# The opening of an encoder kernel: cross-attention key weights loaded as quarters of the inputs instead of one head at a time

## The chip, the cores and the metric

The kernel runs on one core of a Trainium2 chip. The metric is the time of one execution on the device, in microseconds (us). A core has a matrix engine (TensorE, PE in the profile), a vector engine (DVE), a scalar engine (ACT), a sync engine (SP) that here issues nearly all DMA transfers, and 16 DMA engines. Each engine runs its own list of instructions in order. The engines meet only through semaphores.

## The reference, cut to what matters

The program is one layer of a hybrid encoder on 256 tokens of 2048 features. Only its opening is touched by the change. The opening computes, from a second input `mem` (256 tokens of 2048 features), the keys and values of a cross-attention that is used much later:

```python
m = rmsnorm(mem, norm_mem)
kv = (m @ cross_wkv).reshape(1, 256, 2, 4, 128)   # cross_wkv: 2048 x 1024
k, v = kv[:, :, 0], kv[:, :, 1]                   # 4 heads of 128 features each
```

Columns 0 to 511 of `cross_wkv` give the keys, one head per 128 columns, and columns 512 to 1023 give the values. After that the main input `x` is normalised in the same way and multiplied by `w_in`, and the mixers, the output projection, the cross-attention and the feed-forward part follow. All of it is in float32 at full accuracy.

## The kernel before, in words

**Split products.** The kernel multiplies in the format fp32r and keeps the accuracy of float32 by splitting each operand into a high part (a rounding copy) and a low part (operand minus high part), and a product takes three matmuls: high x high, high x low and low x high (`three`, lines 1252 to 1260). A weight chunk is 128 partitions x 2048 floats, 1 MB. For each chunk SP loads it into one of three slots of `raw`, ACT writes the high part `hi` (`split` in the scalar block, line 375), DVE writes the low part `lo` (`split` in the vector block, line 746), and PE multiplies. PE asks for a chunk with `ready(n)`, which waits for the semaphore `lo_ready` that DVE raises. SP may reload a slot when DVE is done with it (`raw_free`), and ACT and DVE may overwrite `hi` and `lo` when PE has finished the chunk three places back (`products_done`).

**The activations.** `mem` is split in the same way, but has to be transposed first, since features must lie on partitions. Features are taken in eight groups of 256 (two 128-blocks k each). `turn_group` (line 1306) has PE transpose a group into a PSUM bank, `token_hi` (line 405) has ACT write the high part times the norm's gain into `uh`, and `token_lo` (line 782) has DVE write the low part into `ul`. The factor 1/rms of each token is applied after the products: DVE computes it (`tile_squares` line 767, `token_rsqrt` line 760 and the lines of `newton`), PE spreads it over the partitions (`spread_scale`, line 1332), and DVE multiplies each head's key block by it when it takes the block out of PSUM (`take_key`, line 864).

**The order of the opening before.** Chunks 0 to 3 are one head each: all 2048 input features x 128 key columns. A DMA of such a chunk reads pieces of 512 bytes. SP issues the four quarters of `mem` with the two halves of chunk 0 between them, waits until all of `mem` has landed, and then issues chunks 1, 2 and 3, the tables and vectors, `x`, and the value chunks 4 to 7. PE turns all eight groups first, each into a bank of its own, and then computes one head after the other, each over all 16 blocks k, into its own bank. The six small transposes of gain and bias vectors (line 1426) follow head 2, and the spreading of 1/rms stands in the middle of it. ACT and DVE split the activations of all groups around the two halves of chunk 0, then chunks 1, 2 and 3 as whole chunks. DVE computes the squares and 1/rms of `mem` between chunks 1 and 3, and those of `x` after chunk 3, with the four `take_key` between the other steps.

**The value part, and what follows.** Chunks 4 to 7 hold quarters of the input features x 512 value columns (pieces of 2048 bytes). `row_product` (lines 1255 to 1257) multiplies each into banks 4 and 5. After each of them PE turns two groups of `x` (`turn_scaled`, line 1325) into the banks that `X_BANKS` names; ACT and DVE split these. In DVE's list, a chain of 18 small operations for the rotary angles (lines 879 to 898) stands between the split of chunk 5 and the split of chunk 6. From chunk 8 on the projection by `w_in` runs one 128-column tile after the other.

The order of all work is written out by hand in one list per engine. No planner decides it.

Of the kernel before, what the change touches and what calls it, by code (L numbers as in the profile page):

```python
# [16 lines left out]
F32, F32R, I32 = mybir.dt.float32, mybir.dt.float32r, mybir.dt.int32  # L17
ALU, ACT, AX = mybir.AluOpType, mybir.ActivationFunctionType, mybir.AxisListType

P = 128  # L20
T = 256
# [70 lines left out]
def products(n):  # L92

    extra = {N_U: 3, N_U + 1: 3, N_U + 2: 6, N_U + 3: 1}
    return n + 1 + sum(v for m, v in extra.items() if m <= n)
# [25 lines left out]
def encoder(nc, x, mem, positions, norm_mix, w_in, mla_q_norm, mla_w_uq, mla_kv_norm, mla_w_ukv, mla_out_norm,  # L121
# [4 lines left out]
    with ctx:  # L126
# [5 lines left out]
        def S(name):  # L132

            if name not in signals:
                signals[name] = Signal(ctx.enter_context(nc.semaphore(name)))
            return signals[name]
# [95 lines left out]
        def _(sp):  # L232
            def raw_free(n):

                sp.wait_ge(S("lo_ready").sem, n - RING + 1)

            def load(n, src, shape, slot=None, off=0):
                slot = n % RING if slot is None else slot
                size = int(np.prod(shape))
                dst = raw[:, slot, off:off + size]  # L240
                if len(shape) == 2:
                    dst = dst.rearrange("p (a b) -> p a b", b=shape[1])
                    sp.dma_start(dst, src).then_inc(S(f"raw_landed{slot}").sem, 16)
                else:
                    dst = dst.rearrange("p (a b c) -> p a b c", b=shape[1], c=shape[2])
                    sp.dma_start(dst, src).then_inc(S(f"raw_landed{slot}").sem, 16)

            def rows(w):
                return w[0].rearrange("(k p) c -> p k c", p=P)

            for q in range(4):
                sp.dma_start(mems[:, :, q * 512:(q + 1) * 512],
                             mem[0].rearrange("(t p) d -> p t d", p=P)[:, :, q * 512:(q + 1) * 512]).then_inc(S(f"mem_landed{q}").sem, 16)
                if q % 2:
                    half = q // 2
                    sp.dma_start(raw[:, 0, half * CH // 2:(half + 1) * CH // 2].rearrange("p (a b) -> p a b", b=P),
                                 rows(cross_wkv)[:, half * KD // 2:(half + 1) * KD // 2, 0:P]).then_inc(
                                     S("raw_landed0" if half else "first_landed").sem, 16)
            for q in range(4):
                sp.wait_ge(S(f"mem_landed{q}").sem, 16)  # L260
            load(1, rows(cross_wkv)[:, :, P:2 * P], (KD, P))
            load(2, rows(cross_wkv)[:, :, 2 * P:3 * P], (KD, P))
            raw_free(3)
            load(3, rows(cross_wkv)[:, :, 3 * P:4 * P], (KD, P))
# [3 lines left out]
            for v, n in ((norm_mix, 16), (norm_cross, 16), (norm_ffn, 16), (mla_q_norm, 4),  # L268
                         (mla_kv_norm, 2), (mla_out_norm, 6), (ssm_norm, 6), (swa_out_norm, 4), (ssm_conv_b, 10)):
                sp.dma_start(vrows[at_row:at_row + n, 0, :], v.rearrange("l (r c) -> (l r) c", c=P)).then_inc(vectors, 16)  # L270
                at_row += n
            sp.dma_start(vrows[0:40, 1, :], ssm_conv_w[0].rearrange("k (r c) -> (k r) c", c=P)).then_inc(vectors, 16)
# [3 lines left out]
            for t in range(TT):  # L276
                sp.dma_start(xs[:, t, :], x[0, t * P:(t + 1) * P, :]).then_inc(S("x_landed").sem, 16)
            sp.dma_start(posi.bitcast(I32), positions[0].partition_broadcast(P)).then_inc(S("pos_landed").sem, 16)
            sp.dma_start(small[:, s_dall:s_dall + SSM_H], ssm_d[0].partition_broadcast(P)).then_inc(S("params_landed").sem, 16)
            sp.dma_start(small[:, s_sink:s_sink + SWA_H], swa_sinks[0].partition_broadcast(P)).then_inc(S("params_landed").sem, 16)  # L280
            sp.dma_start(row12[:, 0:1], ssm_dt_bias.rearrange("l h -> h l")).then_inc(S("params_landed").sem, 16)
            sp.dma_start(row12[:, 1:2], ssm_a_log.rearrange("l h -> h l")).then_inc(S("params_landed").sem, 16)

            for g in range(4):
                raw_free(N_XV + g)
                load(N_XV + g, rows(cross_wkv)[:, 4 * g:4 * g + 4, 512:1024], (4, 512))
# [79 lines left out]
        def _(act):  # L366
# [34 lines left out]
            def token_hi(name, g, g_col, b):  # L401

                act.wait_ge(S(f"{name}_turned").sem, g + 1)
                for k in (2 * g, 2 * g + 1):
                    a.mark(act.activation(uh[:, k, :], bank[b][:, (k % 2) * T:(k % 2 + 1) * T], ACT.Copy,
                                          scale=vecs[:, g_col + k:g_col + k + 1]), S(f"{name}_hi"))
# [62 lines left out]
            for g in range(4):  # L469
                token_hi("mem", g, V_MEM, g)  # L470
            act.wait_ge(S("first_landed").sem, 16)
            a.mark(act.copy(hi[:, 0, 0:CH // 2], raw[:, 0, 0:CH // 2]), S("first_hi"))
            for g in (4, 5):
                token_hi("mem", g, V_MEM, g)
            act.wait_ge(S("raw_landed0").sem, 16)
            a.mark(act.copy(hi[:, 0, CH // 2:], raw[:, 0, CH // 2:]), S("hi_ready"))
            for g in (6, 7):
                token_hi("mem", g, V_MEM, g)

            split(1)  # L480
            a.mark(act.activation(junk, mems[:, 0, :], ACT.Square, accum_out=small[:, s_ss:s_ss + 1]), S("mem_ss"))
            split(2)
            token_root("mem")
            split(3)
            act.wait_ge(S("vecs_turned").sem, 2)
            a.mark(act.copy(vecs[:, 0:V_MEM], bank[3][:, 0:V_MEM]), S("vecs_ready"))
            a.settle()
            act.wait_ge(S("x_landed").sem, 32)
            a.mark(act.activation(junk, xs[:, 0, :], ACT.Square, accum_out=small[:, s_ss:s_ss + 1]), S("x_ss"))
            token_root("x")  # L490
            split(4)
# [239 lines left out]
        def _(dve):  # L731
# [3 lines left out]
            def go(ins, signal=None):  # L735
                d.mark(ins, signal or step)
                d.settle()
# [101 lines left out]
            for g in range(4):  # L839
                token_lo("mem", g, V_MEM, g)  # L840
# [3 lines left out]
            for g in (4, 5):  # L844
                token_lo("mem", g, V_MEM, g)
# [3 lines left out]
            for g in (6, 7):  # L849
                token_lo("mem", g, V_MEM, g)  # L850
            split(1)
            tile_squares("mem", mems)
            split(2)
# [3 lines left out]
            split(3)  # L857
            dve.wait_ge(S("mem_spread").sem, 1)
            go(dve.tensor_copy(mem_scale, bank[4][:, 0:T]))

            def take_key(n):

                dve.wait_ge(S("products_done").sem, products(n))
                d.mark(dve.tensor_tensor(kxT[:, n, :], bank[KEY_BANKS[n]][:, 0:T], mem_scale, ALU.mult), S("key_taken"))

            dve.wait_ge(S("x_landed").sem, 32)
            take_key(0)
# [3 lines left out]
            take_key(1)  # L871
            split(4)
            take_key(2)
            split(5)
            take_key(3)
# [369 lines left out]
        def _(pe):  # L1245
# [162 lines left out]
            for g in range(8):  # L1408
                pe.wait_ge(S(f"mem_landed{g // 2}").sem, 16)
                if g == 7:  # L1410
                    pe.wait_ge(S("vecs_ready").sem, 1)
                turn_group("mem", mems, g, g)
            for n in range(N_XK, N_XK + 4):
                if n == 0:
                    pe.wait_ge(S("first_lo").sem, 1)
                    tile_product(n, n, lo_signal="mem_lo", ks=(0, KD // 2))
                    ready(n)
                    tile_product(n, n, lo_signal="mem_lo", ks=(KD // 2, KD))
                else:
                    ready(n)  # L1420

                    tile_product(n, KEY_BANKS[n], mid=(lambda: spread_scale("mem", mem_diag, 4)) if n == 2 else None)
                if n == 2:
                    pe.wait_ge(S("vectors_landed").sem, N_VECTORS)
                    for k, (r, col) in enumerate(((V_ROWS_A, 0), (40, V_CW), (88, V_FW), (88, V_FW + 88), (88, V_FW + 176), (88, V_FB))):
                        last = pe.transpose(bank[3][:, col:col + r], vrows[0:r, k, :], tab[0:r, C_ID:C_ID + r])
                    last.then_inc(S("vecs_turned").sem, 1)
            for n in range(N_XV, N_XV + 4):
                ready(n)
                g = n - N_XV  # L1430
                row_product(n, uh, ul, 4 * g, 4, g == 0, g == 3)
                if g == 0:
                    pe.wait_ge(S("key_taken").sem, 2)
                    pe.wait_ge(S("vecs_ready").sem, 2)
                if g == 1:
                    pe.wait_ge(S("key_taken").sem, 4)
                if g == 2:
                    pe.wait_ge(S("x_lo").sem, 2)
                if g == 3:
                    pe.wait_ge(S("x_lo").sem, 6)  # L1440
                for gg in (2 * g, 2 * g + 1):
                    turn_scaled("x", xs, x_diag, gg, X_BANKS[gg])
# [285 lines left out]
KEY_BANKS = (0, 1, 2, 7)  # L1728
X_BANKS = (1, 3, 6, 7, 0, 1, 3, 6)
# [11 lines left out]
def z_bank(n):  # L1741
    return n % 3 if n < N_U else (n - N_ZB + 1) % 3

# [52 lines left out]
```

## Time and profile before

| | us |
|---|---|
| median of 3 runs | 1234.81 (1234.19 to 1234.86) |
| the profiled execution | 1234.29 |
| its span in the trace | 1232.5 |
| PE busy | 1200.0 (97% of the span) |
| DVE busy | 884.7 (72%) |
| ACT busy | 655.8 (53%) |
| mean granted clock of TensorE | 0.991 of full speed |

The span is the time from the first to the last recorded instruction; the execution's own time is 1.8 us longer. "Busy" counts the time in which an engine executes something. Start times in all views count from the span's start. The value chunks' matmuls begin at 44.88 us, so the change touches about the first 4% of the span directly.

### The profile page before, as it was taken

How to read it: one execution, taken by the hardware profiler on the slowest of the kernel's cores; microseconds unless marked ns; L12 is line 12 of the kernel's file. 1: busy time of each engine (PE TensorE's matmuls, PEld its weight loads, DVE VectorE, ACT ScalarE, POOL GpSimd, SP SyncE). 2: the span in 40 equal slices, each digit the busy share in tenths (PEclk: the TensorE clock that was granted, in tenths of full speed). 3: DMA queues.
4: the chain of work that ended last, by engine and by line, in shares of the span. 5: the costliest groups of instructions: out<-in, count | busy, mean ns of one | idle time of the engine just before them, and what ended most of it. 6: DMA issues, size and time to landing. Idle time of an engine off the chain costs nothing.

```text
span 1232.5 us, 18921 instructions
## 1 busy us (share of the span) xinstructions
PE 1200.0 (97%) x7020; PEld 1049.7 (85%) x7020; DVE 884.7 (72%) x1243; ACT 655.8 (53%) x866; POOL 0.2 (0%) x4
## 2 busy tenths in 40 slices
PE   7899999999999999999999999999999999999995
PEld 6799999988887888888888888888888888888884
DVE  6763888777476557877767767777777777777775
ACT  6444764475534557646454545555454545454444
POOL 0000000000000000000000000000000000000000
PEclk9999999999899999999999999999999999999998
DMA  8776756442555545766665758575757566575842
GB/s 254 238 180 171 182 155 178 118 114 70 205 171 171 171 137 141 224 185 174 200 192 165 200 168 224 174 204 170 204 172 202 170 191 188 169 202 168 222 152 69
DMA packets 309932, 217.07 MB, mean 176 GB/s; under 512 B 11414, under 2 KB 272254, under 8 KB 309246
## 3 DMA queue, kind: packets, MB, share of 16 engines
q1 hardware_dynamic: 309710, 216.31, 60.7%
q8 instruction: 30, 0.49, 0.2%
q10 hardware_dynamic: 176, 0.14, 0.1%
q14 instruction: 16, 0.13, 0.0%
HBM read 214.33 MB, written 2.10 MB: 176 GB/s over the span
## 4 chain that ended last, share of the span: by engine, by line
PE 92%; DVE 3%; ACT 2%; DMA 2%; issue 1%; SPq 0%; ACTq 0%; DVEq 0%
PE bank L1282 25%; PE bank L1283 12%; PE bank L1255 10%; PE bank L1256 10%; PE bank L1257 10%; PE bank L1258 6%; PE bank L1259 6%; PE bank L1260 6%; PE bank L1286 2%; DVE lo L746 1%; PE bank L1367 1%; DMA raw<-in_cross_wkv_dram 1%; ACT hi L375 1%; PE bank L1398 1%; PE bank L1285 1%; DMA arena<-in_mem_dram 1%
## 5 line engine op out<-in xcount | busy, mean ns | idle before, releaser
L746 DVE TENSOR_TENSOR lo<-raw,hi 128x2048 fp32r<-128x2048 f32 x196 | 448.8, 2290 | 151.1 <-ACT hi L375 143.3
L1282 PE MATMUL bank<-ux,hi 128*128 128x512 f32 x1320 | 470.1, 399 | 0.9 <-DVE arena L1202 0.9
L375 ACT CAST hi<-raw 128x2048 fp32r<-128x2048 f32 x196 | 373.5, 1911 | 111.1 <-PE bank L1257 100.8
L1283 PE MATMUL bank<-ux,lo 128*128 128x256 f32 x1320 | 370.7, 281 | 0.0
L1282 PEld LDWEIGHTS bank<-ux,hi 128*128 128x128 f32 x1320 | 248.0, 188 | 58.7 <-issue 1.2
L1283 PEld LDWEIGHTS bank<-ux,lo 128*128 128x128 f32 x1320 | 249.2, 189 | 4.0
L1255 PE MATMUL bank<-hi,ch 128*128 128x512 f32 x472 | 186.2, 395 | 1.7 <-DVE cl L1142 1.4
L1256 PE MATMUL bank<-lo,ch 128*128 128x512 f32 x472 | 184.7, 391 | 0.0
L1257 PE MATMUL bank<-hi,cl 128*128 128x512 f32 x472 | 184.6, 391 | 0.0
L1258 PE MATMUL bank<-ux,hi 128*128 128x256 f32 (+1 forms) x592 | 170.7, 288 | 1.7 <-DVE lo L746 1.7
L1259 PE MATMUL bank<-ux,hi 128*128 128x256 f32 (+1 forms) x592 | 167.5, 283 | 0.0
L1260 PE MATMUL bank<-ux,lo 128*128 128x256 f32 (+1 forms) x592 | 167.4, 283 | 0.0
L705 ACT COPY arena<-bank 128x256 f32<-128x256 f32 x88 | 32.8, 373 | 208.6 <-PE bank L1286 208.6
L1258 PEld LDWEIGHTS bank<-ux,hi 128*128 128x128 f32 (+1 forms) x592 | 112.9, 191 | 5.2 <-issue 2.4
L1259 PEld LDWEIGHTS bank<-ux,hi 128*128 128x128 f32 (+1 forms) x592 | 112.9, 191 | 0.1
L1260 PEld LDWEIGHTS bank<-ux,lo 128*128 128x128 f32 (+1 forms) x592 | 112.8, 191 | 0.0
L1255 PEld LDWEIGHTS bank<-hi,ch 128*128 128x128 f32 x472 | 89.5, 190 | 20.2 <-DVE cl L1142 1.8
L1257 PEld LDWEIGHTS bank<-hi,cl 128*128 128x128 f32 x472 | 89.6, 190 | 18.9
L1256 PEld LDWEIGHTS bank<-lo,ch 128*128 128x128 f32 x472 | 89.7, 190 | 18.4
L1183 DVE SCALAR_TENSOR_TENSOR arena<-arena,vecs 128x255 f32<-128x255 f32 (+1 forms) x176 | 85.1, 484 | 25.9 <-DVE arena L1202 4.4
L1201 DVE TENSOR_TENSOR arena<-bank,arena 128x256 f32<-128x256 f32 x88 | 37.1, 422 | 62.5 <-ACT arena L705 62.1
L1119 DVE TENSOR_TENSOR arena<-arena,bank 128x512 f32<-128x512 f32 x96 | 60.7, 680 | 0.9 <-PE bank L1257 0.9
(222 smaller groups left out, 1047.2 us busy)
## 6 DMA issues: line engine op xcount, KB each, us to landing
raw<-in_ffn_w_up_dram SPq DMA_DIRECT2D x88, 1024.0 KB, 5.8
raw<-in_ffn_w_down_dram SPq DMA_DIRECT2D x44, 1024.0 KB, 5.1
raw<-in_w_in_dram SPq DMA_DIRECT2D x28, 1024.0 KB, 5.6
raw<-in_w_out_dram SPq DMA_DIRECT2D x16, 1024.0 KB, 5.1
raw<-in_cross_wkv_dram SPq DMA_DIRECT2D x7, 1024.0 KB, 9.2
arena<-in_x_dram SPq DMA_DIRECT2D x4, 1024.0 KB, 5.8
raw<-in_cross_wq_dram SPq DMA_DIRECT2D x4, 1024.0 KB, 5.3
raw<-in_cross_wo_dram SPq DMA_DIRECT2D x4, 1024.0 KB, 5.1
```

What stands on the lines that cost most here:

```text
L375: a.mark(act.copy(hi[:, n % RING, :], raw[:, n % RING, :]), S("hi_ready"))
L746: d.mark(dve.tensor_tensor(lo[:, n % RING, :], raw[:, n % RING, :], hi[:, n % RING, :].bitcast(F32), ALU.subtract), S("lo_ready"))
L1119: d.mark(dve.tensor_tensor(hres[:, t, cb * 512:(cb + 1) * 512], hres[:, t, cb * 512:(cb + 1) * 512], bank[b][:, :], ALU.add), signal)
L1183: go(dve.scalar_tensor_tensor(out=cacc[:, s, tap:T], in0=craw[:, s, 0:T - tap], scalar=vecs[:, bass.ds(col, 1)], in1=cacc[:, s, tap:T], op ...
L1255: pe.matmul(dst, xh, wh, start=start, stop=False)
L1256: pe.matmul(dst, xh, wl, start=False, stop=False)
L1257: return pe.matmul(dst, xl, wh, start=False, stop=stop)
L1258: pe.matmul(dst, wh, xh, start=start, stop=False)
L1259: pe.matmul(dst, wh, xl, start=False, stop=False)
L1260: return pe.matmul(dst, wl, xh, start=False, stop=stop)
L1282: pe.matmul(bank[b][:, :], wh, both_, start=(k == 0), stop=False)
L1283: pe.matmul(bank[b][:, 0:T], wl, uh[:, k, :], start=False, stop=False)
```

## The change

The four key chunks become quarters of the input features x all 512 key columns, like the value chunks. Each quarter of `mem` is issued ahead of its quarter of the weights, and SP no longer waits for `mem`. PE turns only two groups of `mem` (one quarter) before it begins; each further quarter is turned halfway through the products of the quarter before (`turn_mem(q + 1)` at k == 2). The groups use banks 4 to 7 in turn (`mem_bank`). Four key blocks, one per head, fill banks 0 to 3 at the same time and are complete only after the last quarter. ACT and DVE split, for q = 1, 2, 3, first the two groups of `mem` and then the chunk. Squares and 1/rms of `mem` move behind the split of chunk 3 on both engines. On DVE the split of chunk 4, the squares and 1/rms of `x`, the copy of the spread scale, the four key blocks and the split of chunk 5 follow in this order. SP issues chunk 3 behind the tables, and the two tiles of `x` around chunk 4. The diff, complete but for lines of context and a shared indentation:

```diff
@@ -248,20 +248,20 @@
-for q in range(4):
+def load_mem(q):
...
-    if q % 2:
-        half = q // 2
-        sp.dma_start(raw[:, 0, half * CH // 2:(half + 1) * CH // 2].rearrange("p (a b) -> p a b", b=P),
-                     rows(cross_wkv)[:, half * KD // 2:(half + 1) * KD // 2, 0:P]).then_inc(
-                         S("raw_landed0" if half else "first_landed").sem, 16)
-for q in range(4):
-    sp.wait_ge(S(f"mem_landed{q}").sem, 16)
-load(1, rows(cross_wkv)[:, :, P:2 * P], (KD, P))
-load(2, rows(cross_wkv)[:, :, 2 * P:3 * P], (KD, P))
-raw_free(3)
-load(3, rows(cross_wkv)[:, :, 3 * P:4 * P], (KD, P))
+load_mem(0)
+for half in range(2):
+    sp.dma_start(raw[:, 0, half * CH // 2:(half + 1) * CH // 2].rearrange("p (a b) -> p a b", b=512),
+                 rows(cross_wkv)[:, 2 * half:2 * half + 2, 0:512]).then_inc(
+                     S("raw_landed0" if half else "first_landed").sem, 16)
+for q in (1, 2):
+    load_mem(q)
+    load(q, rows(cross_wkv)[:, 4 * q:4 * q + 4, 0:512], (4, 512))
+load_mem(3)
...
@@ -269,19 +269,21 @@
+raw_free(3)
+load(3, rows(cross_wkv)[:, 12:16, 0:512], (4, 512))
...
-for t in range(TT):
-    sp.dma_start(xs[:, t, :], x[0, t * P:(t + 1) * P, :]).then_inc(S("x_landed").sem, 16)
-sp.dma_start(posi.bitcast(I32), positions[0].partition_broadcast(P)).then_inc(S("pos_landed").sem, 16)
-sp.dma_start(small[:, s_dall:s_dall + SSM_H], ssm_d[0].partition_broadcast(P)).then_inc(S("params_landed").sem, 16)
-sp.dma_start(small[:, s_sink:s_sink + SWA_H], swa_sinks[0].partition_broadcast(P)).then_inc(S("params_landed").sem, 16)
-sp.dma_start(row12[:, 0:1], ssm_dt_bias.rearrange("l h -> h l")).then_inc(S("params_landed").sem, 16)
-sp.dma_start(row12[:, 1:2], ssm_a_log.rearrange("l h -> h l")).then_inc(S("params_landed").sem, 16)
...
+    if g < TT:
+        sp.dma_start(xs[:, g, :], x[0, g * P:(g + 1) * P, :]).then_inc(S("x_landed").sem, 16)
+    if g == 2:
+        sp.dma_start(posi.bitcast(I32), positions[0].partition_broadcast(P)).then_inc(S("pos_landed").sem, 16)
+        sp.dma_start(small[:, s_dall:s_dall + SSM_H], ssm_d[0].partition_broadcast(P)).then_inc(S("params_landed").sem, 16)
+        sp.dma_start(small[:, s_sink:s_sink + SWA_H], swa_sinks[0].partition_broadcast(P)).then_inc(S("params_landed").sem, 16)
+        sp.dma_start(row12[:, 0:1], ssm_dt_bias.rearrange("l h -> h l")).then_inc(S("params_landed").sem, 16)
+        sp.dma_start(row12[:, 1:2], ssm_a_log.rearrange("l h -> h l")).then_inc(S("params_landed").sem, 16)
...
@@ -466,29 +468,26 @@
-for g in range(4):
-    token_hi("mem", g, V_MEM, g)
+for g in (0, 1):
+    token_hi("mem", g, V_MEM, mem_bank(g))
...
-for g in (4, 5):
-    token_hi("mem", g, V_MEM, g)
...
-for g in (6, 7):
-    token_hi("mem", g, V_MEM, g)
-split(1)
+for q in (1, 2, 3):
+    for g in (2 * q, 2 * q + 1):
+        token_hi("mem", g, V_MEM, mem_bank(g))
+    split(q)
...
-split(2)
...
-split(3)
-act.wait_ge(S("vecs_turned").sem, 2)
-a.mark(act.copy(vecs[:, 0:V_MEM], bank[3][:, 0:V_MEM]), S("vecs_ready"))
+split(4)
+act.wait_ge(S("x_landed").sem, 32)
...
-act.wait_ge(S("x_landed").sem, 32)
...
-split(4)
+act.wait_ge(S("vecs_turned").sem, 2)
+a.mark(act.copy(vecs[:, 0:V_MEM], bank[6][:, 0:V_MEM]), S("vecs_ready"))
+a.settle()
...
@@ -836,43 +835,33 @@
-for g in range(4):
-    token_lo("mem", g, V_MEM, g)
+for g in (0, 1):
+    token_lo("mem", g, V_MEM, mem_bank(g))
...
-for g in (4, 5):
-    token_lo("mem", g, V_MEM, g)
...
-for g in (6, 7):
-    token_lo("mem", g, V_MEM, g)
-split(1)
+for q in (1, 2, 3):
+    for g in (2 * q, 2 * q + 1):
+        token_lo("mem", g, V_MEM, mem_bank(g))
+    split(q)
...
-split(2)
...
-split(3)
-dve.wait_ge(S("mem_spread").sem, 1)
-go(dve.tensor_copy(mem_scale, bank[4][:, 0:T]))
-def take_key(n):
-    dve.wait_ge(S("products_done").sem, products(n))
-    d.mark(dve.tensor_tensor(kxT[:, n, :], bank[KEY_BANKS[n]][:, 0:T], mem_scale, ALU.mult), S("key_taken"))
+split(4)
...
-take_key(0)
...
-take_key(1)
-split(4)
-take_key(2)
+dve.wait_ge(S("mem_spread").sem, 1)
+go(dve.tensor_copy(mem_scale, bank[7][:, 0:T]))
+dve.wait_ge(S("products_done").sem, products(3))
+for j in range(X_H):
+    d.mark(dve.tensor_tensor(kxT[:, j, :], bank[j][:, 0:T], mem_scale, ALU.mult), S("key_taken"))
...
-take_key(3)
...
@@ -1405,37 +1394,50 @@
-for g in range(8):
-    pe.wait_ge(S(f"mem_landed{g // 2}").sem, 16)
-    if g == 7:
-        pe.wait_ge(S("vecs_ready").sem, 1)
-    turn_group("mem", mems, g, g)
-for n in range(N_XK, N_XK + 4):
-    if n == 0:
+def turn_mem(q):
+    pe.wait_ge(S(f"mem_landed{q}").sem, 16)
+    for g in (2 * q, 2 * q + 1):
+        if g == 3:
+            pe.wait_ge(S("vecs_ready").sem, 1)
+        if g >= 4:
+            pe.wait_ge(S("mem_lo").sem, 2 * (g - 4) + 2)
+        turn_group("mem", mems, g, mem_bank(g))
+turn_mem(0)
+for q in range(4):
+    if q == 0:
...
-        tile_product(n, n, lo_signal="mem_lo", ks=(0, KD // 2))
-        ready(n)
-        tile_product(n, n, lo_signal="mem_lo", ks=(KD // 2, KD))
...
-        ready(n)
-        tile_product(n, KEY_BANKS[n], mid=(lambda: spread_scale("mem", mem_diag, 4)) if n == 2 else None)
-    if n == 2:
-        pe.wait_ge(S("vectors_landed").sem, N_VECTORS)
-        for k, (r, col) in enumerate(((V_ROWS_A, 0), (40, V_CW), (88, V_FW), (88, V_FW + 88), (88, V_FW + 176), (88, V_FB))):
-            last = pe.transpose(bank[3][:, col:col + r], vrows[0:r, k, :], tab[0:r, C_ID:C_ID + r])
-        last.then_inc(S("vecs_turned").sem, 1)
+        ready(q)
+    for k in range(4):
+        if k == 2:
+            if q == 0:
+                ready(0)
+            if q < 3:
+                turn_mem(q + 1)
+            else:
+                pe.wait_ge(S("vectors_landed").sem, N_VECTORS)
+                for m, (r, col) in enumerate(((V_ROWS_A, 0), (40, V_CW), (88, V_FW), (88, V_FW + 88), (88, V_FW + 176), (88, V_FB))):
+                    last = pe.transpose(bank[6][:, col:col + r], vrows[0:r, m, :], tab[0:r, C_ID:C_ID + r])
+                last.then_inc(S("vecs_turned").sem, 1)
+        kk_ = 4 * q + k
+        pe.wait_ge(S("mem_lo").sem, 2 * (kk_ // 2) + 2)
+        for j in range(X_H):
+            o = k * 512 + j * P
+            last = three(bank[j][:, 0:T], hi[:, q % RING, o:o + P], lo[:, q % RING, o:o + P], uh[:, kk_, :], ul[:, kk_, :],
+                         kk_ == 0, kk_ == KD - 1)
+    last.then_inc(done, 1)
+spread_scale("mem", mem_diag, 7)
...
-        pe.wait_ge(S("key_taken").sem, 2)
+        pe.wait_ge(S("key_taken").sem, 1)
...
-    if g == 2:
-        pe.wait_ge(S("x_lo").sem, 2)
...
@@ -1725,8 +1727,7 @@
-KEY_BANKS = (0, 1, 2, 7)
-X_BANKS = (1, 3, 6, 7, 0, 1, 3, 6)
+X_BANKS = (6, 7, 2, 3, 0, 1, 6, 7)
...
@@ -1740,6 +1741,11 @@
+def mem_bank(g):
+    return 4 + g % 4
...
```

## Rows read from the trace of the kernel before

**Rows 1.** The page: busy time of the engines, and who held the chain that ended last.

```profile
PE 1200.0 (97%) x7020; PEld 1049.7 (85%) x7020; DVE 884.7 (72%) x1243; ACT 655.8 (53%) x866; POOL 0.2 (0%) x4
...
PE 92%; DVE 3%; ACT 2%; DMA 2%; issue 1%; SPq 0%; ACTq 0%; DVEq 0%
```

**Rows 2.** Timeline of PE: start, duration (us), line, operation, count, [idle before and releaser].

```profile
5.55 1.97 PE L1306 MATMUL bank<-tab,arena 128*128 128x128 f32 x8
...
10.89 3.67 PE L1306 MATMUL bank<-tab,arena 128*128 128x128 f32 x16 [0.95 <-DMA arena<-in_mem_dram]
...
22.29 0.38 PE L1258 MATMUL bank<-ux,hi 128*128 128x256 f32 x1 [1.73 <-DVE lo L746]
...
25.27 0.28 PE L1258 MATMUL bank<-ux,hi 128*128 128x256 f32 x1
...
34.35 0.87 PE L1426 MATMUL bank<-tab,arena 80*128 80x80 f32 x6
...
44.88 0.50 PE L1255 MATMUL bank<-hi,ux 128*128 128x512 f32 x1 [3.88 <-DVE lo L746]
...
52.07 1.95 PE L1325 MATMUL bank<-arena 128*128 128x128 f32 x16
...
53.77 0.48 PE L1255 MATMUL bank<-hi,ux 128*128 128x512 f32 x1
...
61.03 0.48 PE L1255 MATMUL bank<-hi,ux 128*128 128x512 f32 x1
```

**Rows 3.** Timeline of ACT, same columns.

```profile
6.76 1.63 ACT L405 ACTIVATE ux<-bank,vecs 128x256 fp32r<-128x256 f32 x4 [0.94 <-PE bank L1306]
...
10.70 1.04 ACT L472 CAST hi<-raw 128x1024 fp32r<-128x1024 f32 x1
...
12.04 1.69 ACT L405 ACTIVATE ux<-bank,vecs 128x256 fp32r<-128x256 f32 x4 [0.29 <-PE bank L1306]
...
13.67 1.05 ACT L476 CAST hi<-raw 128x1024 fp32r<-128x1024 f32 x1
...
40.60 1.90 ACT L375 CAST hi<-raw 128x2048 fp32r<-128x2048 f32 x1 [2.24 <-DMA raw<-in_cross_wkv_dram]
```

**Rows 4.** Timeline of DVE, same columns.

```profile
7.73 1.66 DVE L782 SCALAR_TENSOR_TENSOR ux<-bank,vecs,ux 128x256 fp32r<-128x256 f32 x4 [7.73 <-ACT ux L405]
...
11.78 1.22 DVE L842 TENSOR_TENSOR lo<-raw,hi 128x1024 fp32r<-128x1024 f32 x1
...
22.15 2.28 DVE L767 CUSTOM_DVE_ANT_0 arena<-arena 128x2048 f32<-128x2048 f32 x1
...
26.69 0.16 DVE L760 TENSOR_SCALAR small<-small 128x2 f32<-128x2 f32 x1
...
28.98 2.29 DVE L746 TENSOR_TENSOR lo<-raw,hi 128x2048 fp32r<-128x2048 f32 x1 [0.23 <-DVE mem_r L856]
...
39.85 0.42 DVE L864 TENSOR_TENSOR arena<-bank,arena 128x256 f32<-128x256 f32 x1
...
49.03 0.28 DVE L879 CAST arena<-arena 128x256 f32<-128x256 int32 x1
...
56.63 2.29 DVE L746 TENSOR_TENSOR lo<-raw,hi 128x2048 fp32r<-128x2048 f32 x1
```

**Rows 5.** Stretches: length, busy time per engine, granted clock, DMA share, GB/s.

```profile
0.00:9.60 9.60, 3.82 (x17) 3.32 (x17) 1.66 (x4) 3.56 (x8) 0.20 (x4) 1.00 0.79 234
...
16.50:24.00 7.50, 5.77 (x48) 5.57 (x48) 5.10 (x5) 5.97 (x5) 0.00 (x0) 1.00 1.19 290
...
38.00:44.00 6.00, 3.00 (x26) 2.80 (x24) 3.22 (x10) 2.10 (x2) 0.00 (x0) 1.00 1.05 397
...
46.00:48.00 2.00, 2.00 (x6) 1.57 (x5) 1.51 (x1) 1.29 (x2) 0.00 (x0) 0.50 0.78 266
...
342.00:344.00 2.00, 2.00 (x8) 1.56 (x7) 1.90 (x6) 1.23 (x1) 0.00 (x0) 0.67 0.42 162
```

**Rows 6.** Timeline of PE ahead of a later fall of the clock.

```profile
338.27 2.74 PE L1339 MATMUL bank<-tab,arena 128*128 128x1 f32 x24
```


## The prediction

> **What bounds the kernel now.** I read the page first. PE is busy for 97% of the span and holds 92% of the chain that ended last [rows 1]. So a change in the opening is worth what it moves the moment from which PE runs without a gap. The timeline of PE shows that moment. Its key products start, then stop once for 1.73 us before head 1, waiting for DVE's low part of a chunk; they end at about 41.0, and PE idles 3.88 us more until the first value chunk is split, at 44.88 [rows 2]. The timeline of ACT says why: the cast of that chunk waited 2.24 us for the DMA and began at 40.60 [rows 3]. After the 3.88 us the granted clock fell to 0.50 for a while [rows 5]; value chunk 4 took 52.07 - 44.88 = 7.19 us, while chunk 5 takes 61.03 - 53.77 - 1.70 = 5.56 us, where 1.70 is the turning of x, 53.77 - 52.07 [rows 2]. The difference, 1.63 us, is what one fall of the clock costs here when PE has work. From 53.77 on PE has no gap in this part. My mark is the start of value chunk 6 at 61.03: whatever moves it moves the end, because no work or order behind it is changed.
>
> **The start of the products.** PE turns one quarter of mem instead of four. The first quarter is turned from 5.55, as now, to about 7.5 [rows 2]. ACT's four high parts begin at 6.76 and take 1.63, so the cast of the first half chunk can begin at 8.39 and takes 1.04, to 9.43 [rows 3]. DVE ends its four low parts at 7.73 + 1.66 = 9.39 and the half chunk's low part takes 1.22 [rows 4], so PE starts at 10.75. The first product began at about 14.2 before (10.89 plus the turning of two quarters). The cost of this is a wait of PE of 10.75 - 7.5 = 3.2 us.
>
> **The loads.** Pieces become 2048 instead of 512 bytes. Rows at hand: 290 GB/s while only 512-byte pieces moved, 397 GB/s with long ones [rows 5]. Queue order up to the first half chunk is 1.2 MB with the constants, up to mem quarter 1 2.24 MB, up to chunk 1 3.3 MB. By 9.6 us 9.6 x 234 = 2.25 MB had moved, and PE's wait for the same amount ended at 10.89 [rows 2, 5], so landing lags by 1.3 us. Chunk 1 then lands at 9.6 + 1.05/0.397 + 1.3 = 13.5 (14.5 at 290 GB/s). It is needed at 16.5 (below). All later loads have more room: chunk 3 waits at SP only for the first split, x and the value chunks each follow a split by 10 us or more. I cost the loads at zero, with a cover of 2 us. SP has no wait on mem any more, and the small vector DMAs that now stand ahead of chunk 3 are needed only at 44.
>
> **The rhythm of a quarter.** This is the term that decides. PE turns quarter q+1 halfway through quarter q, and both ACT and DVE have the two groups of mem ahead of the chunk in their lists. So the split of chunk q+1 can't begin before PE has turned, although the chunk landed long before. Let T be the start of the turning. ACT begins at T + 1.15 (12.04 against 10.89 [rows 2, 3]); its four high parts occupy it for 13.67 - 12.04 = 1.63; the cast takes 1.91 [rows 3]; DVE's low part takes 2.29 [rows 4]; with 0.06 to reach PE, ready(q+1) comes at T + 7.05. PE in the meantime turns (3.67/2 = 1.84) and does half a quarter, 24 matmuls, which take 25.27 - 22.29 = 2.98 [rows 2]. It is done at T + 4.8 and idles 2.2 us. Then it does the other 24 matmuls and turns again: the period is 7.05 + 2.98 = 10.03 us where PE's own work is 7.8. The three periods hold 6.7 us of idle time that is not there now.
> With PE at full clock: T1 = 10.75 + 2.98 = 13.73, ready(1) 20.8, T2 = 23.8, T3 = 33.8, DVE done with chunk 3 at 40.8. PE ends the keys at 40.8 + 2 x 2.98 + 0.87 for the vectors [rows 2] = 47.6, and is at the first value chunk near 48.1 with the spreading, for which I allow 0.5.
>
> **DVE's list behind chunk 3.** Before, the squares and 1/rms of mem lay beside head products, and those of x while PE still had head 3. Now all of it stands in one line between chunk 3 and chunk 6, with durations from [rows 4]: squares of mem 2.3; 1/rms and diagonal 2.29 (28.98 - 26.69), to 45.4; chunk 4 2.29, to 47.7; squares of x 2.3; 1/rms and diagonal 1.9 (the same less a copy of 0.4), to 51.9; scale copy and four key blocks 5 x 0.42 less overlap, 1.9, to 53.8; chunk 5 2.29, to 56.1; the rotary chain 56.63 - 49.03 = 7.6, to 63.7; chunk 6 2.29, to 66.0. That is 25.2 us from 40.8. PE's own way to chunk 6 is 48.1 + 5.56 + 1.70, wait for chunk 5 until 56.1, + 5.56 + 1.70 = 63.4, so it waits 2.6 us for DVE. ACT is not in the way: its cast of chunk 4 is done by 45.3 and that of chunk 5 by 52.8. PE's new wait for the first key block costs nothing, as it is there at 52.7, before 53.7. Value chunk 6 begins at 66.05 instead of 61.03: 5.0 us later. Chunks 7 and 8 are split by 70 and 74, before PE asks at 73.3 and 80.6, so nothing is added and nothing is given back.
>
> **The clock.** What short waits do to it is not shown directly. From below: the wait of 1.73 us brought no fall, the clock of 16.5 to 24 us is 1.00 [rows 5]. From above: 3.88 us did, for 1.63 us of loss, and a fall also came inside 342 to 344 us behind 2.74 us of one-column matmuls, with next to no idle time [rows 5, 6]. The change brings a wait of 3.2 us and four or five of 2.2 to 2.6. So the cost lies between 0 and 5 x 1.63 = 8.2 us, less the part that DVE's line hides anyway. Less than zero it can't be: the fall of before, behind the 3.88 us, lies ahead of my mark and is already taken back with it. I take one full fall for the wait of 3.2 us, which lies nearest to 3.88 (it falls on the first half quarter and delays T1), and half of one, 0.8, for the others together: 2.4.
> The Trainium skill, "TensorE: Matmul & The Clock Gate", section "HAM oscillation — how this bites in real kernels", warns only of idle gaps longer than any that I forecast; by that rule no fall comes. The trace speaks against it with the fall at 342.
>
> **Sum.** 5.0 + 2.4 = 7.4 us on the profiled execution's 1234.29 (span 1232.5 and 1.8 around it): 1241.7. That execution lies 0.5 below the median of the runs, so I say 1242.0.
>
> **The rivals.**
> (a) The order as above, but no fall of the clock: 1234.5 + 5.0 = 1239.5. For it: 1.73 us of idle left the clock alone. Against: 3.2 us is near 3.88, and the fall at 342 had hardly a gap.
> (b) Falls after nearly every wait: each of the first three delays the next T by up to 1.63, the one before chunk 6 adds as much: 5.0 + 4 x 1.63 = 11.5, 1246. Waits of 2.2 us filled up to 10 us by work speak against it.
> (c) Faster: the rhythm does not set DVE's pace and PE goes through without idling. One mechanism: chunk q+1 is split before PE turns, so that ready(q+1) costs nothing. Then the keys would end at 10.75 + 8 x 2.98 + 3 x 1.84 + 0.87 + 0.5 = 41.5 without the wait for DMA, DVE would be done with chunk 3 about 33, chunk 6 follows 25.2 us later at 58.3, and the kernel comes to 1234.5 - 2.7 = 1231.8. The point from which it decides: DVE must be done with chunk 3 before 61.0 - 25.2 = 35.8, 5 us earlier than I have it, or 1.7 us less per period. The program order of both lists speaks against it; for it, the start 3.5 us earlier and the idle of 3.88 us that is gone.
> (d) Loads land later than computed, as the first 9.6 us moved only 234 GB/s: each us of chunk 1 behind 16.5 adds one, 1243 to 1245.
> (e) DVE's line is shorter than the sum by overlaps and the rhythm holds: about 1235, no change.
>
> **Chances.** Forecast (one to three falls, 1240 to 1244) 0.48; (a) 0.22; (b) 0.13; (c) 0.09, with a little of it inside no change; (d) 0.04; (e) 0.04. A difference under 0.2%, 2.5 us, can't be told from none by this measurement. Faster 0.08, same 0.04, slower 0.88. The range, 1238 to 1246, holds the forecast, (a), (d) and most of (b), and leaves out (c) and (e).
>
> **What would show it.** In the new trace PE's first key product is at 10.7; each later quarter waits about 2.2 us for line 746's low part, with quarters 10 us apart; ACT idles before each pair of high parts and waits for PE, no longer for the DMA; value chunk 4 starts at 48 to 50 and chunk 6 at 66 to 69 with a wait for DVE ahead of it; the granted clock falls once after 11 us. It is wrong if chunk 6 begins before 62, if a chunk's cast starts before its mem groups, or if ACT's casts wait for the DMA.

## The result, and the profile after

The changed kernel takes 1240.29 us (median of 6 runs, 1238.38 to 1242.55) against 1234.50 (6 runs) of the kernel before: a ratio of 1.005, 95% interval 1.0034 to 1.0067. A second series gave 1241.28 against 1233.40, ratio 1.0077, interval 1.0064 to 1.0090. It is slower, by 5.8 us in the one series and 7.9 in the other. The profiled execution took 1242.55 us, 8.3 more than that of before.

The page first, its chain of waits by engine. PE still holds it; ACT and DVE gained a share, and the share of the DMA, 2% before [rows 1], is gone:

```profile
PE 91%; DVE 4%; ACT 3%; issue 1%; DMA 0%; ACTq 0%; DVEq 0%
```

PE's timeline of the changed kernel (start, duration, line, operation, count, idle before and what ended it). In this kernel these lines stand 11 lower than before (each experiment has line numbers of its own): L1295 turns mem, L1247 is the first matmul of a key product, L1244 that of a value product, L1314 turns x:

```profile
6.02 1.97 PE L1295 MATMUL bank<-tab,arena 128*128 128x128 f32 x8
...
11.10 0.58 PE L1247 MATMUL bank<-ux,hi 128*128 128x256 f32 x1 [3.12 <-DVE lo L841]
...
16.39 1.09 PE L1295 MATMUL bank<-tab,arena 128*128 128x128 f32 x8
...
22.82 0.39 PE L1247 MATMUL bank<-ux,hi 128*128 128x256 f32 x1 [2.48 <-DVE lo L745]
...
27.29 1.04 PE L1295 MATMUL bank<-tab,arena 128*128 128x128 f32 x8
...
33.67 0.58 PE L1247 MATMUL bank<-ux,hi 128*128 128x256 f32 x1 [2.48 <-DVE lo L745]
...
38.09 1.03 PE L1295 MATMUL bank<-tab,arena 128*128 128x128 f32 x8
...
44.46 0.39 PE L1247 MATMUL bank<-ux,hi 128*128 128x256 f32 x1 [2.47 <-DVE lo L745]
...
51.42 0.47 PE L1244 MATMUL bank<-hi,ux 128*128 128x512 f32 x1
...
59.50 0.50 PE L1244 MATMUL bank<-hi,ux 128*128 128x512 f32 x1 [0.57 <-DVE lo L745]
...
69.33 0.50 PE L1244 MATMUL bank<-hi,ux 128*128 128x512 f32 x1 [2.32 <-DVE lo L745]
```

These answer to [rows 2]. The products start 3.1 us earlier, but from each turning (L1295) to the next products pass 6.4 us, with a wait of 2.48 for the chunk's low part. Key products end at about 51.0 instead of 41.0, and chunk 6, my mark, starts at 69.33 instead of 61.03: 8.30 us, all of the difference between the two profiled executions (8.26). What lies behind the mark took 1234.29 - 61.03 = 1173.26 before and 1242.55 - 69.33 = 1173.22 now.

ACT, quarter 1 (answers to [rows 3]): it idles until PE has turned, and only then casts the chunk, which had landed long before (by 12.34 us in e1, whose loads are the same):

```profile
17.08 1.57 ACT L407 ACTIVATE ux<-bank,vecs 128x256 fp32r<-128x256 f32 x4 [6.34 <-PE bank L1295]
18.52 1.93 ACT L377 CAST hi<-raw 128x2048 fp32r<-128x2048 f32 x1
```

DVE (answers to [rows 4]). Between chunk 3 and chunk 6 it has no wait over 0.34 us:

```profile
42.12 2.29 DVE L745 TENSOR_TENSOR lo<-raw,hi 128x2048 fp32r<-128x2048 f32 x1 [0.86 <-ACT hi L377]
44.33 2.28 DVE L766 CUSTOM_DVE_ANT_0 arena<-arena 128x2048 f32<-128x2048 f32 x1
...
48.95 2.29 DVE L745 TENSOR_TENSOR lo<-raw,hi 128x2048 fp32r<-128x2048 f32 x1 [0.23 <-DVE mem_r L853]
...
57.17 2.28 DVE L745 TENSOR_TENSOR lo<-raw,hi 128x2048 fp32r<-128x2048 f32 x1
59.37 0.29 DVE L868 CAST arena<-arena 128x256 f32<-128x256 int32 x1
...
66.98 2.29 DVE L745 TENSOR_TENSOR lo<-raw,hi 128x2048 fp32r<-128x2048 f32 x1
```

Stretches of the changed kernel (length, busy times of PE, PEld, DVE, ACT, POOL with counts, granted clock, DMA share, GB/s; answers to [rows 5]). The clock fell behind the first two of the waits of 2.48 us, not behind the third:

```profile
12.00:14.00 2.00, 2.00 (x11) 2.00 (x11) 0.18 (x1) 0.00 (x0) 0.00 (x0) 1.00 1.05 409
24.00:26.00 2.00, 2.00 (x11) 2.00 (x11) 0.00 (x0) 0.00 (x0) 0.00 (x0) 0.50 0.78 262
34.00:36.00 2.00, 2.00 (x11) 2.00 (x11) 0.00 (x0) 0.00 (x0) 0.00 (x0) 0.50 0.55 105
```

The first of these rows says 1.00, yet it holds 11 matmuls in 2 us, as many as the two rows at 0.50: the products up to 16.39 ran at half speed too, and the clock column does not show it.

### The profile page after: what moved, and what is told of

Same layout as the page of the kernel before. It is cut to its first block, busy times and chain, and to the rows that moved or that the text cites. A ratio compares the mean times of both kernels' runs of the same rounds, so it can differ in the third digit from the quotient of the medians.

```text
span 1241.0 us, 18922 instructions
## 1 busy us (share of the span) xinstructions
PE 1201.6 (97%) x7020; PEld 1051.4 (85%) x7020; DVE 884.7 (71%) x1243; ACT 655.2 (53%) x866; POOL 0.2 (0%) x4
## 4 chain that ended last, share of the span: by engine, by line
PE 91%; DVE 4%; ACT 3%; issue 1%; DMA 0%; ACTq 0%; DVEq 0%
PE bank L1271 25%; PE bank L1272 12%; PE bank L1244 9%; PE bank L1246 9%; PE bank L1245 9%; PE bank L1247 6%; PE bank L1248 6%; PE bank L1249 6%; DVE lo L745 2%; PE bank L1275 2%; ACT hi L377 1%; PE bank L1356 1%; PE bank L1387 1%; PE bank L1274 1%; PE bank L1328 1%
## 5 line engine op out<-in xcount | busy, mean ns | idle before, releaser
L1244 PE MATMUL bank<-hi,ch 128*128 128x512 f32 x472 | 186.2, 395 | 1.7 <-DVE cl L1131 1.4
L1247 PE MATMUL bank<-ux,hi 128*128 128x256 f32 (+1 forms) x592 | 173.5, 293 | 10.5 <-DVE lo L745 7.4
L1248 PE MATMUL bank<-ux,hi 128*128 128x256 f32 (+1 forms) x592 | 169.8, 287 | 0.0
L1247 PEld LDWEIGHTS bank<-ux,hi 128*128 128x128 f32 (+1 forms) x592 | 115.1, 194 | 14.8 <-DVE lo L745 8.0
L1248 PEld LDWEIGHTS bank<-ux,hi 128*128 128x128 f32 (+1 forms) x592 | 115.3, 195 | 0.1
L1244 PEld LDWEIGHTS bank<-hi,ch 128*128 128x128 f32 x472 | 89.5, 190 | 20.3 <-DVE cl L1131 1.8
```

The lines of the kernel that those rows point to most:

```text
L1244: pe.matmul(dst, xh, wh, start=start, stop=False)
L1247: pe.matmul(dst, wh, xh, start=start, stop=False)
L1248: pe.matmul(dst, wh, xl, start=False, stop=False)
```

## The experiments

The mark (start of chunk 6) and what lies behind it, from each kernel's trace, and the time of that same execution:

| kernel | chunk 4 starts | chunk 6 starts | execution | behind the mark |
|---|---|---|---|---|
| before | 44.88 | 61.03 | 1234.29 | 1173.3 |
| changed | 51.42 | 69.33 | 1242.55 | 1173.2 |
| again (changed) | 50.50 | 66.90 | 1238.33 | 1171.4 |
| e1_chunk_first | 39.45 | 56.93 | 1228.48 | 1171.6 |
| e2_rotary_late | 51.09 | 65.61 | 1238.67 | 1173.1 |
| e3_filler | 46.26 | 64.16 | 1237.41 | 1173.3 |
| e4_rms_early | 51.49 | 66.02 | 1239.11 | 1173.1 |
| e5_order | 40.53 | 55.06 | 1226.79 | 1171.7 |
| e6_order_fill | 38.21 | 52.74 | 1224.44 | 1171.7 |
| e7_before_fill | 45.22 | 59.76 | 1232.94 | 1173.2 |

The last column takes two values, about 1171.6 and 1173.2. So an execution is its opening plus one of two levels. Ratios hold each kernel against runs of the kernel before in its own series: 1233.40 us (17 runs) for again, e1, e2 and e3, and 1232.82 (17 runs) for e4 to e7.

**again: the changed kernel once more.** No edit.

> The changed kernel unaltered, for a second trace and as the level that the others are held against. Its runs so far fall into two groups, 1238.4 to 1238.7 and 1241.9 to 1242.6. Theory (clock): the groups differ by whether the clock falls behind the 2.5 us waits; then this trace, if its time is near 1238.5, shows fewer matmuls of quarter 1 and 2 at a spacing of 0.21 us than the first trace (24 matmuls took 4.47 and 4.42 us there, 2.98 at full clock), and if it is near 1242 it shows the same. Rival: the groups differ somewhere behind the opening; then value chunk 6 starts at 69.3 us in both.

Measured: 1241.28 (1238.33 to 1242.90, 5 runs). The trace is of an execution of 1238.33. Both theories hold a part. In the opening the clock fell after the waits before quarters 1 and 3, not 2; the fall in quarter 3 was hidden, since DVE's line sets chunk 6. The slow start was shorter too: the first 24 matmuls took 15.62 - 10.98 = 4.64 us instead of 5.29. The mark came 2.4 us earlier. Behind the mark 1.8 us more are gone. The stretch from 320 to 360 us, first of the changed kernel's first trace, then of this one, has a mean clock of 0.87 and 0.91, that is one slow stretch fewer:

```profile
320.00:360.00 40.00, 39.55 (x194) 33.58 (x193) 19.50 (x31) 21.75 (x28) 0.00 (x0) 0.87 0.58 208
```

```profile
320.00:360.00 40.00, 39.55 (x198) 33.55 (x197) 23.55 (x37) 22.52 (x27) 0.00 (x0) 0.91 0.59 211
```

The two levels of the last column come from there. Added up over windows of 1 us, the half clock takes 5.1 us between 262 and 295 us behind the mark in every trace of the high level and 3.4 us in every trace of the low one. In this trace and in that of e1 one slow stretch of two stays away; in e5 and e6 both are there, but the first is shorter. One unaltered kernel shows both levels, so a level belongs to the execution, and 1.7 us of a difference between two traces can come from it alone. Whether an edit makes one level more frequent is not shown.

**e1_chunk_first: only the order within ACT's and DVE's lists.** The same edit in both:

```diff
 for q in (1, 2, 3):
+    split(q)
     for g in (2 * q, 2 * q + 1):
         token_hi("mem", g, V_MEM, mem_bank(g))      # DVE: token_lo
-    split(q)
```

> ACT and DVE split chunk q ahead of the two mem groups of quarter q. Theory (rhythm of the quarter): the three waits of 2.5 us are gone, key products end near 40.5 instead of 51, value chunk 6 starts near 58.5 (DVE's line of 25 us from about 33.2) instead of 69.3, and the kernel comes to 1232 (1230 to 1234), faster than the kernel before. Rival (the start and the clock, not the lists, cost the time): the waits stay and the time stays at 1238 to 1242. Rival (the loads are what holds the splits back): ACT's casts wait for the DMA and the time is above 1236.

Measured: 1228.88 (12 runs), ratio 0.9972 of the kernel before, interval 0.9963 to 0.9982. PE has no wait between 11.15 and the end of the keys; from turning to turning pass 6.62 us, where the changed kernel takes 10.9:

```profile
15.61 1.03 PE L1295 MATMUL bank<-tab,arena 128*128 128x128 f32 x8
22.23 1.03 PE L1295 MATMUL bank<-tab,arena 128*128 128x128 f32 x8
...
56.93 0.50 PE L1244 MATMUL bank<-hi,ux 128*128 128x512 f32 x1 [2.32 <-DVE lo L745]
```

ACT waits for chunk 1 until it lands at 12.34, the one wait for a load, and PE has no wait that comes of it:

```profile
12.34 1.90 ACT L377 CAST hi<-raw 128x2048 fp32r<-128x2048 f32 x1 [1.56 <-DMA raw<-in_cross_wkv_dram]
```

The rhythm of the quarter is what made the change slower: moving one line in each of two lists takes 12.4 us from the mark of the first trace (10.0 from that of the second) and turns the change into a gain. The 12.4 us hold the waits and the falls of the clock that followed them; of the clock's cost only the slow start is left, 15.61 - 11.15 - 2.98 = 1.5 us. Both rivals fall: the waits did not stay, and the one wait for a load did not hold PE up. The time is lower than the 1230 to 1234 expected: chunk 6 starts 1.6 us earlier than 58.5, since DVE took up its line behind quarter 3 at 31.9 instead of 33.2, and the execution has the low level.

**e2_rotary_late: the rotary chain behind the split of chunk 6.**

```diff
 split(5)
-<chain of 18 operations for the rotary angles>
 for n in range(N_XV, N_XV + 4):
     ...
     split(n + 2)
+    if n == N_XV:
+        <chain of 18 operations for the rotary angles>
```

> The chain of 18 small DVE operations for the rotary angles stands behind the split of chunk 6 instead of ahead of it, all else as in the changed kernel. Theory (DVE's line holds chunk 6): the wait of 2.3 us before chunk 6 is gone, chunk 6 starts at 66.8 against 69.3, and the time falls by 2.5 us, to 1236 to 1240. Rival (PE would have been late anyway, or chunk 7 now waits for the same chain): under 0.5 us gained.

Measured: 1238.67 (1237.46 to 1240.00), ratio to before 1.0051, against 1.0077 of the unaltered changed kernel in the same series. In the trace chunk 6 starts 14.52 us behind chunk 4, which is two products and two turnings (2 x 7.26) and no wait; it is 17.91 in the changed kernel's first trace. That is not the fair measure: the trace of e2 has its falls before quarters 1 and 3, as again has, where DVE gets ahead of PE. Against again (16.40 us from chunk 4 to chunk 6) the edit gives 1.9 us:

```profile
66.90 0.53 PE L1244 MATMUL bank<-hi,ux 128*128 128x512 f32 x1 [1.63 <-DVE lo L745]
```

```profile
65.61 0.48 PE L1245 MATMUL bank<-hi,ux 128*128 128x512 f32 x1
```

The wait for DVE (first row, again) is gone in e2 (second row), so DVE's line held chunk 6. The times alone do not prove it: the two intervals meet at 1.0064, and the first series gave the unaltered kernel 1.005.

**e3_filler: PE kept busy in its waits.** The results of the added transposes are not used. `...` stands for the lines left out.

```diff
 turn_mem(0)
 for q in range(4):
+    for _ in range(13 if q == 0 else 18):
+        pe.transpose(bank[6 if q == 0 else mem_bank(2 * q - 2)][:, 0:P], ident, ident)
     ...wait for first_lo or ready(q)
```

> PE gets extra 128x128 transposes of the identity into a free bank: 13 before the first key product and 18 before each of the three later quarters; their results are used by nobody. Theory (clock): the waits stay as long in us, but quarters 1 and 2 run their first 24 matmuls in 3.0 us instead of 4.4, and part of the first 24 runs at full clock, so chunk 6 starts 3 to 5 us earlier and the time is 1235.5 to 1239.5 without the two groups. Rival (the slow matmuls come from four banks or from the loads that run at the same time): the spacing stays at 0.21 us and the time is not lower than 1238.4, or higher by the extra work.

Measured: 1237.16 (1235.61 to 1238.70), ratio to before 1.0037 (1.0025 to 1.0049), against 1.0077 (1.0064 to 1.0090) unaltered in the same series. No fall in the opening; the first 24 matmuls take 14.21 - 11.17 = 3.0 us, those of quarter 1 23.57 - 20.60 = 3.0:

```profile
11.17 0.45 PE L1247 MATMUL bank<-ux,hi 128*128 128x256 f32 x1 [0.35 <-DVE lo L841]
...
14.21 1.04 PE L1295 MATMUL bank<-tab,arena 128*128 128x128 f32 x8
...
17.96 2.13 PE L1410 MATMUL bank<-tab 128*128 128x128 f32 x18
...
20.60 0.39 PE L1247 MATMUL bank<-ux,hi 128*128 128x256 f32 x1 [0.51 <-DVE lo L745]
...
23.57 1.03 PE L1295 MATMUL bank<-tab,arena 128*128 128x128 f32 x8
```

The same products on the same four banks beside the same loads run at full speed once PE is kept busy. So it is the clock, and the mark of this kernel tells the two costs apart: 69.33 - 64.16 = 5.2 us come from the clock in the first trace, and 64.16 - 61.03 = 3.1 are left. These 3.1 are not the price of the order by itself, because the 61.03 of the kernel before hold its own fall of 1.6 us ahead of the mark. With no fall on either side the order would cost about 4.7 us; this is an estimate, 64.16 - (61.03 - 1.61), with 7.19 - 5.58 from e7.

**e4_rms_early: squares and 1/rms of mem ahead of quarter 3.**

```diff
 for q in (1, 2, 3):
+    if q == 3: <wait for mem; squares and 1/rms of mem>       # ACT and DVE
     <groups of mem>; split(q)
-<squares and 1/rms of mem>
```

> The changed kernel with the squares and 1/rms of mem ahead of quarter 3 on ACT and DVE instead of behind chunk 3; groups still ahead of chunks. Theory (DVE's line behind chunk 3): DVE idles 6 us there anyway, its line is 4.6 us shorter, chunk 5 is ready in time and chunk 6 starts when PE gets there, 3.2 us earlier than in the changed kernel with the same falls of the clock; time 1235.5 to 1239.5. The waits of 2.5 us per quarter stay. Rival (PE's late end of the keys alone sets chunk 6): under 1 us gained.

Measured: 1238.81 (1237.60 to 1240.77), ratio to before 1.0051. The opening has the same two falls as the first trace and chunk 4 starts at the same time (51.49), but no wait follows: chunk 6 starts at 66.02, 3.3 us earlier, as expected. With the same falls in both, this trace is the clean proof that DVE's line held chunk 6:

```profile
66.02 0.48 PE L1250 MATMUL bank<-hi,ux 128*128 128x512 f32 x1
```

It overlaps with e2: either edit is enough to free chunk 6.

**e7_before_fill: the price of a fall, in the kernel before.** 32 transposes of the identity into bank 5 ahead of chunk 4.

> The kernel before with 32 transposes of the identity on PE, used by nobody, in the wait of 3.9 us between the last key product and chunk 4. Theory (that wait costs a fall of the clock, 1.63 us): chunk 4 takes 5.56 instead of 7.19 us and the time is 1.6 us lower than before, ratio 0.9987. Rival (the slow stretch has another cause): chunk 4 keeps its 7.2 us and the time does not change.

Measured: 1231.97 (11 runs) against 1232.82, ratio 0.9992, interval 0.9982 to 1.0001. By times alone that is unclear, though the expected 0.9987 lies in the interval. The trace shows the mechanism: chunk 4 takes 50.80 - 45.22 = 5.58 us instead of 7.19.

```profile
41.81 3.66 PE L1429 MATMUL bank<-tab 128*128 128x128 f32 x32
45.22 0.47 PE L1255 MATMUL bank<-hi,ux 128*128 128x512 f32 x1
50.80 1.95 PE L1325 MATMUL bank<-arena 128*128 128x128 f32 x16
```

This execution had another fall at 23 to 27 us instead, behind the wait before head 1, which was 2.83 us long here and 1.73 in the first trace.

**e5_order and e6_order_fill: put together.** e5 is e1 plus e2, and the squares of mem (not the 1/rms) stand between the split of chunk 3 and the groups of quarter 3. e6 adds the 13 transposes ahead of the first product.

> Chunk ahead of groups as in e1_chunk_first, squares of mem between the split of chunk 3 and the groups of quarter 3, rotary chain behind chunk 6. Theory: e1_chunk_first still waited for DVE ahead of chunk 5 (0.4 us) and chunk 6 (2.6 us); both go, chunk 6 starts at 54.0 instead of 56.96, and the time is 3 us below e1_chunk_first: 1226 (1225 to 1228). Rival (what is behind chunk 6 gives it back, since the rotary chain now holds chunk 7): the same 1229 as e1_chunk_first.

> e5_order plus 13 transposes of the identity on PE, used by nobody, before the first key product. Theory (PE starts the keys at half clock because it had been idle): the first 24 matmuls take 3.0 instead of 5.3 us... in e1_chunk_first they took 4.5; so 1.5 to 2 us less than e5_order, 1224. Rival (the slow start has to do with the loads that run beside it, or the next wait is for chunk 1 to land, which ACT waited for until 12.34): no gain over e5_order.

Measured: e5 1226.35 (1225.59 to 1226.79), ratio 0.9946, interval 0.9933 to 0.9959; e6 1224.03 (1223.89 to 1224.55), ratio 0.9929, interval 0.9916 to 0.9942. Both beat the kernel before, and by their ratios the changed one. No run of e6 is above 1224.55 and none of e5 below 1225.59, so the 2.3 us between them are clear. In e5 chunk 6 starts 14.53 us behind chunk 4, without a wait. In e6 chunk 4 starts 2.3 us earlier than in e5: the first 24 matmuls take 14.37 - 11.14 = 3.2 us instead of 5.3 (16.49 - 11.21). The slow start of e5 is a long one; e1's took 4.5 us, so part of the gain depends on the execution.

## Why the prediction was right, point by point

1242.0 was forecast, slower, within 1238 to 1246; 1240.29 was measured. The mechanism was the one named, and the rivals (a) to (e) did not occur. The size, though, came out near by luck: two errors cancel, the order costing less than forecast and the clock more. The forecast put the mark 7.4 us later; the two traces have it 8.3 and 5.9 later.

- **Start of the products**: 10.75 forecast, 11.10 measured. The constants landed at 5.80 instead of 5.33; the wait of 3.2 us is there (3.12).
- **Loads at zero**: right. In the opening no engine of the changed kernel waits for a DMA behind 6 us. Chunk 1 landed at 12.3 (e1), not 13.5, and was asked for at 18.52, so the cover was 6 us.
- **Rhythm of the quarter** (from T, the start of a turning, to the next quarter's first product): T + 7.05 forecast, T + 6.43, 6.38 and 6.37 measured. The mis-sized term is ACT's start, T + 1.15: it is 0.69 (17.08 - 16.39). The row I took it from [rows 2, 3] was itself at half clock: eight transposes take 1.8 us there and 0.8 here. PE's wait is 2.48 against 2.2, since its own turning is shorter too.
- **DVE's line**: 25.2 us forecast from the end of chunk 3 to chunk 6, 69.27 - 44.41 = 24.9 measured; chunk 5's wait 0.57 and chunk 6's 2.32, forecast 0.7 (56.1 - 55.4) and 2.6. e2 and e4 confirm it from two sides.
- **Order together**, against the mark of the kernel before with its fall: 5.0 us forecast, 3.1 shown by e3, where no fall disturbs. The three chains are 2.0 shorter and DVE's line 0.3, and the start is 0.4 later.
- **The clock**: 2.4 us forecast, 5.2 in the first trace: 16.39 - 11.10 - 2.98 = 2.3 for the slow start, 1.5 and 1.4 for quarters 1 and 2. I had reasoned from one fall behind the wait of 3.1 us; in fact PE was not at full clock before it either, its eight transposes taking 1.8 us, and e3 and e6 show that work in that wait brings the products to full speed. The step that failed is the reading of 1.00 in the clock column of the opening [rows 5] as full speed. The number of later falls was right as a range, 2 in both traces, one of them hidden in the second; each cost 1.4 to 1.5 us, where the prediction gave all later waits 0.8 together.

With these sizes the sum closes: 10.75 + 2.98 + 3 x 7.05 + 2 x 2.98 = 40.84 forecast for ready(3), the moment when quarter 3's chunk is split; + 0.35 for the start, - 1.97 for three shorter chains, + 5.24 for the clock gives 44.46, and 44.46 was measured.

The rule of the Trainium skill weighed in the prediction ("TensorE: Matmul & The Clock Gate", section "HAM oscillation — how this bites in real kernels"), by which waits as short as these cause no fall, is contradicted here: waits of 2.47 to 2.49 us were followed by a fall in eight of twelve cases (the first trace, again, e2 and e4, two of three in each), and e3, which fills them, has none. The waits of 2.3 us ahead of chunk 6 (the first trace, e1, e3) were followed by none.

Rival (c), priced at 1231.8, did not occur in the change, but its mechanism is exactly what e1 built: chunks split before the groups, 1228.9.

## What to carry to other kernels

When an engine's work for step q+1 depends on something that PE does in the middle of step q, work that does not depend on it should not stand behind it in that engine's list. Order a list by what is ready first, not by what is used first; e1 did no more than this. Price waits of PE from the trace with their clock, and check a recorded clock of 1.00 against the spacing of matmuls of known size before taking a duration from there. Where executions of one kernel fall into groups, split each at a fixed mark; here that separated the opening from slow stretches 262 to 295 us behind the mark.

## What the runs showed that was not expected

At the start of an execution the granted clock is recorded as 1.00 while matmuls of 256 columns follow each other at 0.21 us instead of 0.12, and 128x128 transposes at 0.22 instead of 0.10. How long this lasts varies: the first 24 matmuls took 4.5 us in e1, 4.6 in again, 4.9 in e2 and 5.3 in the first trace, e4 and e5, against 2.98 at full speed. Keeping PE busy from 6 us on, with work that nobody uses, brought the first products to full speed and gained 2.3 us of 1226.4 (e5 to e6). A wait of PE of 2.48 us was followed by a slow stretch sometimes and sometimes not, in the same kernel at the same place. What decides it was not tested. The two traces of the changed kernel reach these waits 0.8, 1.0 and 2.4 us apart, and behind different stretches of slow and fast clock.
